# The first matmul group on a layer norm's output, with feature chunks as the outer loop and four PSUM banks as the inner one

## What is computed

```
def decoder_layer(x, pos, lp, past):
    x = layer_norm(ALPHA * x + 0.5 * swiglu(x, lp['ffn_wg'][0], lp['ffn_wu'][0], lp['ffn_wd'][0]), lp['ln_g'][0], lp['ln_b'][0])
    y, st = token_mixing(x, pos, lp, past)
    x = layer_norm(ALPHA * x + y, lp['ln_g'][1], lp['ln_b'][1])
    x = layer_norm(ALPHA * x + 0.5 * swiglu(x, lp['ffn_wg'][1], lp['ffn_wu'][1], lp['ffn_wd'][1]), lp['ln_g'][2], lp['ln_b'][2])
    return x, st
```

## Time and profile before

| what | us |
|---|---|
| median of 3 runs | 1693.02 |
| lowest, highest | 1691.62, 1695.55 |
| span of the profiled execution (first to last instruction) | 1688.6 |
| PE busy in it | 1534.0 |
| DVE busy | 833.3 |
| ACT busy | 524.3 |

### The profile page before, as it was taken

One profiled execution on the slowest core, in us unless ns is written; L12 is line 12 of the kernel. 1 busy time (PEld: TensorE's weight loads), 2 busy tenths in 40 slices (PEclk: granted clock), 3 DMA queues, 4 the chain that ended last, 5 costly groups with the idle time before them and its releaser, 6 DMA issues.

```text
span 1688.6 us, 25683 instructions
## 1 busy us (share of the span) xinstructions
PE 1534.0 (91%) x10092; PEld 1263.3 (75%) x10092; DVE 833.3 (49%) x1575; ACT 524.3 (31%) x772; POOL 94.6 (6%) x159
## 2 busy tenths in 40 slices
PE   7999989999887889999899998999998878899994
PEld 6999965565554569999799997754745456799994
DVE  5555476543424236554565545765442334555543
ACT  3433252112212125333344333330321222433331
POOL 8000010010000010000100001001000000100001
PEclk9999989966789899999999999999587889999997
DMA  8555744374051133556635557334801402356550
GB/s 272 182 169 144 197 139 139 118 210 112 1 162 39 51 100 120 180 168 158 198 119 184 168 155 228 111 115 145 231 7 52 149 1 70 94 187 192 144 138 26
DMA packets 254702, 226.88 MB, mean 134 GB/s; under 512 B 12468, under 2 KB 234818, under 8 KB 254466
## 3 DMA queue, kind: packets, MB, share of 16 engines
q1 hardware_dynamic: 250402, 220.86, 44.2%
q0 software_dynamic: 4192, 4.56, 0.9%
HBM read 221.52 MB, written 3.86 MB: 133 GB/s over the span
## 4 chain that ended last, share of the span: by engine, by line
PE 83%; DVE 8%; ACT 3%; SPq 2%; issue 2%; DMA 1%; POOL 0%; DVEq 0%; ACTq 0%
PE bank L588 18%; PE bank L666 18%; PE bank L668 17%; PE bank L667 17%; PE bank L959 2%; PE bank L783 2%; PE bank L846 2%; PE bank L675 1%; PE bank L676 1%; PE bank L811 1%; ACT x L1080 1%; SPq L406 1%; DVE rstd L1569 1%; DVE rstd L1364 1%; SPq L407 1%
## 5 line engine op out<-in xcount | busy, mean ns | idle before, releaser
L666 PE MATMUL bank<-x_high,w_low 128*128 128x264 f32 x1408 | 405.6, 288 | 28.0 <-DVE x_low L1302 23.9
L667 PE MATMUL bank<-x_low,w_high 128*128 128x264 f32 x1408 | 402.5, 286 | 0.0
L668 PE MATMUL bank<-x_high,w_high 128*128 128x264 f32 x1408 | 402.3, 286 | 0.0
L1320 DVE TENSOR_TENSOR w_low<-weights,w_high 128x2048 fp32r<-128x2048 f32 (+1 forms) x172 | 347.7, 2039 | 72.0 <-ACT w_high L1059 56.6
L666 PEld LDWEIGHTS bank<-x_high,w_low 128*128 128x128 f32 x1408 | 268.6, 191 | 32.0 <-issue 28.0
L667 PEld LDWEIGHTS bank<-x_low,w_high 128*128 128x128 f32 x1408 | 269.3, 191 | 0.0
L668 PEld LDWEIGHTS bank<-x_high,w_high 128*128 128x128 f32 x1408 | 267.7, 190 | 0.0
L666 PE MATMUL bank<-hidden_high,w_low 128*128 128x264 f32 x704 | 205.0, 291 | 0.0
L668 PE MATMUL bank<-hidden_high,w_high 128*128 128x264 f32 x704 | 199.9, 284 | 0.0
L667 PE MATMUL bank<-hidden_low,w_high 128*128 128x264 f32 x704 | 198.9, 283 | 0.0
L1101 ACT ACTIVATE w_high<-weights 128x2048 fp32r<-128x2048 f32 (+1 forms) x88 | 163.8, 1862 | 10.2 <-DMA weights<-in_ffn_wu_dram 10.2
(11 more groups left out here) (290 smaller groups left out, 2015.1 us busy)
## 6 DMA issues: line engine op xcount, KB each, us to landing
weights<-in_ffn_wg_dram SPq DMA_DIRECT2D x44, 1024.0 KB, 5.5
weights<-in_ffn_wu_dram SPq DMA_DIRECT2D x44, 1024.0 KB, 8.0
weights<-in_ffn_wd_dram SPq DMA_DIRECT2D x64, 704.0 KB, 6.3
weights<-in_w_in_dram SPq DMA_DIRECT2D x20, 1024.0 KB, 5.3
bc_pages<-in_cache_bc_kv_dram SPq DMA_DIRECT2D x128, 128.0 KB, 2.1
ring<-in_cache_bs_kv_dram SPq DMA_DIRECT2D x128, 128.0 KB, 2.1
ring<-in_cache_bw_kv_dram SPq DMA_DIRECT2D x16, 512.0 KB, 4.1
weights<-in_w_out_dram SPq DMA_DIRECT2D x16, 512.0 KB, 11.1
```

The source lines that it names most:

```text
L666: mm(out, w_low, v_high, start=start, stop=False)
L667: mm(out, w_high, v_low, start=False, stop=False)
L668: return mm(out, w_high, v_high, start=False, stop=stop)
L1320: tt(low(k, half), raw(k, half), high(k, half).bitcast(F32), ALU.subtract).then_inc(low_done, 1)
```

## The change

At five of the six places of a run where x enters such a group of four banks, the loops over chunks and banks change places: for each chunk c all four banks get their three matmuls, and only then is the next chunk waited for. In `ffn` a new function `opening` does so for the first group when f > 0. In `mix` the four banks are claimed first, and the three `compress` calls that stood after m = 1, 2 and 3 stand one after another behind the last chunk. The five are f = 1, 2, 3 and the mixing stage of both layers. ACT's, DVE's, SP's and GpSimd's programs are the same as before.

```diff
-                                if isinstance(n0, int) and n0 + q + i == 0:
+                                if f == 0 and isinstance(n0, int) and n0 + q + i == 0:
                                     pe.wait_ge(low_x_ready, (3 * l + 2 * j) * KC + c + 1)
...
-                for g in range(SLOTS):
+                def opening(k):
+
+                    pe.wait_ge(hidden_done, f * FC)
+                    pe.wait_ge(low_done, halves_before(l, k) + 2)
+                    halves = [[w(k, i).rearrange("p (c f) -> p c f", c=KC) for w in (high, low)] for i in range(2)]
+                    for c in range(KC):
+                        pe.wait_ge(low_x_ready, (3 * l + 2 * j) * KC + c + 1)
+                        for q in range(2):
+                            for (wh, wl), full in zip(halves, (gate_full, up_full)):
+                                last = product(banks[2 * q + (full is up_full)][:, 0:TOK], wh[:, c, q * P:(q + 1) * P],
+                                               wl[:, c, q * P:(q + 1) * P], x_high[:, c, :], x_low[:, c, :],
+                                               c == 0, c == KC - 1)
+                                if c == KC - 1:
+                                    last.then_inc(full, 1)
+
+                if f:
+                    opening(base)
+                else:
+                    group(base, halves_before(l, base), 0)
+                for g in range(1, SLOTS):
                     group(base + g, halves_before(l, base + g), 2 * g)
...
-                for m in range(4):
-                    out = bank_v() if m < 2 else bank_a()
-                    for c in range(KC):
-                        if m == 0:
-                            pe.wait_ge(low_x_ready, (3 * l + 1) * KC + c + 1)
-                        last = product(out[:, 0:TOK], *parts_of(k, c, slice(m * P, (m + 1) * P)),
+                outs_f = [bank_v(), bank_v(), bank_a(), bank_a()]
+                for c in range(KC):
+                    pe.wait_ge(low_x_ready, (3 * l + 1) * KC + c + 1)
+                    for m in range(4):
+                        last = product(outs_f[m][:, 0:TOK], *parts_of(k, c, slice(m * P, (m + 1) * P)),
                                        mix_x_high[:, c, :], mix_x_low[:, c, :], c == 0, c == KC - 1)
-                    last.then_inc(v_full if m < 2 else a_full, 1)
-                    if m:
-                        compress()
+                        if c == KC - 1:
+                            last.then_inc(v_full if m < 2 else a_full, 1)
+                for m in range(3):
+                    compress()
```

## The result

The changed kernel takes **1700.74 us** (median of 4 runs, 1699.64 to 1702.56). The kernel before, run beside it, took 1694.22 (4 runs, 1691.62 to 1695.55). The ratio is 1.0046, with a 95% interval of 1.0032 to 1.006: slower, by 0.46%. The forecast was 1701.8. The profiled execution took 1699.64 us and has a span of 1697.9, against 1688.6 for that of before. What lies around a span is thus 1.7 us, and 1.7 to 1.8 in every other run that is on record with its span, not the 4.4 by which the median of before stood above its span. By that, the profiled execution of before took some 1690.4 us (an estimate), less than any of its runs beside the result. This is why the spans differ by more, 9.3 us, than these medians, 6.5.

What follows compares the result with a forecast made beforehand. PE, with 83% of the chain of waits, was taken as the bound. Mixing stages +6.4, clock +4.5 and FFNs -2.1 gave +8.8 us: span 1697.4, plus 4.4 for the median, 1701.8; range 1695.5 to 1707.0.

Steps and rivals of the forecast that it cites:

- The sign and the sum: Whole kernel: slower, with mixing stages +6.4, clock +4.5 and FFNs -2.1 making +8.8 us on the span.
- The likeliest case: Whole kernel: the forecast itself, stops in both mixing stages with the clock fallen behind them, 1701.8 us; chance 0.70.
- The opening: First 96 matmuls at each of five places: 14.0 us, with 5.0 us of it at the lower clock.
- The FFNs: Three later FFN openings: gains of 0.25, 1.65 and 0.25 after a new wait, 2.1 us together.
- The wait behind silu and copy: FFN group 1: PE waits 0.75 us for the split half of its weights, since silu starts later.
- The stop: Mixing stages: PE stands still before page group 2 for its refetched buffer, 5.5 us in layer 0, 5.7 in layer 1.
- The clock behind it: After PE's standstill before page group 2: clock fallen, back after 5.0 us of dense work, costing 2.25 us per layer.
- A (no cost): Mixing stages: later waits absorb the page groups' delay, or refetch fits within 1.84 us; faster, 1686.1 us; chance 0.06.
- B (the clock stays up): Mixing stages: PE stands still before page group 2 but the clock does not fall; +4.3, 1697.3 us; chance 0.15.
- C (the bank change keeps the clock low): Openings and restarts: changing bank every three matmuls makes lower-clock stretches 8.9 us; +12.3, 1714 us; chance 0.04.
- D (a longer wait in the FFNs): FFNs: the wait exceeds 0.75 us and takes the whole 4.4 gained by three openings; 1704 us; chance 0.05.
- Page groups 3 to 15 keep their distances to group 2: Mixing stages, after page group 2: later page groups keep their spacing, so the loss is passed on.

Runs made afterwards that it cites:

- e2_clump_only: Kernel before with only the three page groups of each mixing stage moved behind the fourth bank, old bank order kept; 1707.79 us, ratio 1.0086.
- e1_ffn_only: Changed kernel with the mixing stage of before, so only the three FFN openings are new; 1689.64 us, ratio 0.9979 of before.
- e3_fill: Changed kernel with 42 unread matmuls more per layer between page groups 1 and 2; 1697.45 us, ratio 1.003 of before.
- e4_page0_chunk3: Changed kernel with page group 0 behind the fourth of eight chunks, groups 1 and 2 behind the last; 1682.39 us, ratio 0.9941 of before.
- e5_page0_chunk6: Changed kernel with page group 0 behind the seventh of eight chunks, groups 1 and 2 behind the last; 1698.44 us, ratio 1.0037 of before.
- after once more: Changed kernel run again unchanged, beside the others on one chip; 1701.65 us, ratio 1.0053 of before.
- e6_early_halves: e4_page0_chunk3 with both halves of group 1's weights copied and split ahead of first silu and product in three later FFNs; 1681.68 us, ratio 0.9935 of before.

## Why the prediction was right, step by step

**The sign and the sum.** +8.8 us were forecast on the span; the span grew by 9.3, the medians by 6.5 and 8.7. The likeliest case came about. That the sum fits better than its terms is in part luck: the two mixing stages lost 12.3 us where 10.9 were forecast, the FFNs gained 2.4 where 2.1 were, and 0.7 us were gained in stretches that the change does not touch. So is the nearness of the median: the 4.4 us added to the span were not what lies around it, and the changed kernel's median stands 2.8 above its span.

**The opening** was put at 14.0 us with 5.0 us at the lower clock. In after it is 14.1 (layer 0), 14.3 (layer 1) and 14.2 (f = 1). The windows place the clock's rise 5.0, 5.2, 3.2, 5.4 and 5.2 us after the first matmul. Only f = 2 differs: 3.2, so it gained more than forecast. The choice of 5.0 between 4.1 and 8.9 was less well founded than it reads. PE did not wait between chunks the whole time in f = 2 of before: the windows from 843 to 851 have it busy for 7.96 of 8 us, and from 849.28 to the clock's rise the starts lie 0.22 us apart.

```profile
848.51 0.42 PE L668 MATMUL bank<-x_high,w_high 128*128 128x264 f32 x1
848.90 0.59 PE L666 MATMUL bank<-x_high,w_low 128*128 128x264 f32 x1
...
849.50 0.42 PE L668 MATMUL bank<-x_high,w_high 128*128 128x264 f32 x1
849.72 0.42 PE L666 MATMUL bank<-x_high,w_low 128*128 128x264 f32 x1
```

In all 33 openings of the new order that have a trace the rise came between 3.1 and 6.1 us after the first matmul; with the old order it came only after 8.6 to 9.0 us at two of the five places of before and at three of the five of `e2_clump_only`. So that the late rise goes with the old order is borne out; that five openings average near 5.0 is in part luck.

**The FFNs** were to gain 2.1: -0.25, -1.65 and -0.25. The trace shows +0.06, -2.20 and -0.22, so 2.4; `e1_ffn_only`, where nothing else moved, 2.7 in the medians. It hangs on the clock at f = 2: in `e3_fill`, `e4_page0_chunk3` and `e5_page0_chunk6`, where it came up there 6.0 us after the first matmul, the three FFNs gained 1.5 to 1.8. The wait behind silu and copy was put at 0.75 us. The chain came as forecast, by the timelines of ACT and DVE at f = 1, where the opening ends at 653.15; they answer to the earlier trace rows:

```profile
652.23 0.39 ACT L1126 ACTIVATE shared<-bank 128x264 f32<-128x264 f32 x1 [4.64 <-PE bank L687]
652.52 1.91 ACT L1120 ACTIVATE w_high<-weights 128x2048 fp32r<-128x2048 f32 x1
```

```profile
654.46 2.29 DVE L1339 TENSOR_TENSOR w_low<-weights,w_high 128x2048 fp32r<-128x2048 f32 x1 [0.57 <-ACT w_high L1120]
```

Silu starts 0.9 us ahead of the opening's end, the copy 0.3 behind it, and the split ends at 656.75, 3.6 us after the opening, as worked out. The price is 0.64.

**The stop** was put at 5.5 and 5.7 us and is 5.68 and 5.62. Page group 2 starts 23.44 and 23.58 us after the first matmul where it started 19.32 and 20.69 before: 4.1 and 2.9 lost, forecast 3.8 and 2.6. `e4_page0_chunk3` removes it, `e5_page0_chunk6` shortens it by the work that now stands between groups 0 and 1 and leaves the time from group 0 to group 2 as it was, `e2_clump_only` has it without the rest of the change: that the refetch of the first buffer sets it is shown.

**The clock behind it** was put at 2.25 us per layer. From page group 2's start to group 6 the loss grows by another 2.6 (6.72 - 4.12) and 2.7 (5.60 - 2.89). The term was 0.4 short, since the clock took 5.5 us to return and not 5.0 (in layer 1 5.75), and a us at the lower clock cost 0.47 there and not 0.45. The other runs bear this price out. From page group 2 to page group 6 it is 34.18 us in both layers of before. After the same stop `e2_clump_only` has 1.95 and 1.7 us more, with 4.1 and 3.6 us at the lower clock behind PE's restart; `e5_page0_chunk6` 1.6 and 1.3 more, with 3.4 and 2.7 us; `e3_fill`, where the clock stays up, nothing. So what the clock takes behind such a stop went from 1.3 to 2.7 us, by how much of the lower clock lay behind the restart.

**The rivals.** A (no cost) is out: 5.7 us at page group 2. B (the clock stays up) is out: 0.50 in the windows, and `e3_fill`, which holds the clock up, has page group 2 at 1.91 us and the 2.6 and 2.7 us back. C (the bank change keeps the clock low) did not happen: the clock rose 3.2 to 5.4 us into five openings that change bank every three matmuls. The Trainium skill, TensorE: Matmul & The Clock Gate, A second HAM failure mode: psum-queue depth-cycling, tells of a kernel whose clock swung because TensorE idled between groups as it cycled through banks; in these traces such cycling, with no gaps between the banks, was no hindrance. D (a longer wait in the FFNs) is out: 0.64 us.

**What did not come as written** is a smaller step: "Page groups 3 to 15 keep their distances to group 2, so the loss is passed on". In layer 0 the stretch behind page group 6 was 1.0 us shorter. That is not the loss given back: `e1_ffn_only`, which has no stop, took 349.15 us there too. The table under the last heading has that stretch some 2 us longer or shorter in kernels that do not differ in it, so a forecast from one trace could hold it no more closely.

## What to carry to other kernels

Work that stands between two parts of a loop may be the cover of somebody's refetch: before loops change places, ask of each buffered tile how long lies between its last use and the next use of the same buffer, and hold that against the length of the refetch (here 7.3 us against 1.84 left). Of a stop on TensorE, count the stop itself and the lower clock behind it, here 5.6 us and 1.7 to 2.7 more. A loop order can be right and its side effect the loss: taken apart, the bank order gained and the moved page groups lost, and one line put page group 0 back under cover.

## What was not expected of the hardware

The same instructions, from page group 6 of a layer to the first matmul of the next FFN, took these times (us) in the profiled executions:

| kernel | layer 0 | layer 1 |
|---|---|---|
| before | 350.17 | 349.39 |
| after | 349.17 | 349.33 |
| after once more | 349.17 | 349.42 |
| `e1_ffn_only` | 349.15 | 351.67 |
| `e2_clump_only` | 351.82 | 349.34 |
| `e3_fill` | 349.25 | 350.74 |
| `e4_page0_chunk3` | 347.79 | 349.68 |
| `e5_page0_chunk6` | 350.06 | 347.69 |
| `e6_early_halves` | 347.20 | 349.35 |

That is 4.6 us between kernels that do not differ there. The two traced executions of the changed kernel agree within 0.1 us, but the runs of one kernel spread too, and the longer ones show a lower mean granted clock: of the 20 runs of before on one chip the shortest, 1690.17 us, has 0.911, the longest, 1699.15, has 0.903. The stretch shows the same. Added up over windows of 1 us, the clock was at its lower level for 112.0 to 114.3 us in the three shortest (347.20, 347.69 and 347.79) and for 124.5 in the two longest (351.67 and 351.82); the others have 115 to 121. So a longer stretch goes with more time at the lower clock. The stretch has many waits of 1 to 4 us on PE. I take it that the clock falls in other ones of these waits when the stage begins at another moment; no run here tested that, and it stays open. `e4_page0_chunk3` owes to it some 2 us of what it gained on before.

The second is that in `e5_page0_chunk6` the clock fell for a stop of 3.75 us, and fell at 254.2, 0.8 us after PE had taken up its work again, while in `e4_page0_chunk3` and `e3_fill`, where the stop was gone, it stayed up. A stop can thus be paid for after it is over.
